# Expert stage of a hybrid decoder layer: the down products of a tile are placed between the two halves of the next tile's gate and up products

## What is computed

```python
g_sel = argmax(h @ w_group + b)            # one of 4 groups per token
top_v, top_i = top_k(e_in, 2)              # two of the 4 experts of that group
hg = einsum('td,edf->tef', t, w_gate)      # 1024 -> 256 per expert
hu = einsum('td,edf->tef', t, w_up)        # 1024 -> 256 per expert
act = silu(hg) * hu * comb
out = einsum('tef,efd->td', act, w_down)   # 256 -> 1024 per expert
return h + out
```

## Time and profile before

| what | value |
|---|---|
| median of 3 runs | 1578.01 us (1574.78 to 1580.17) |
| profiled execution, its own time | 1579.26 us |
| span of that execution in the trace | 1577.2 us |
| PE busy over the span | 1460.0 us, 93% |
| DVE busy | 1093.0 us, 69% |
| ACT busy | 770.2 us, 49% |
| first transposes of an activation (tile 0), start | 1245.40 us |
| transposes of the activation of tile 29, start | 1547.69 us |
| last product of the kernel, start | 1561.24 us |

### The profile page before, as it was taken

The page is one execution under the profiler, slowest core; times in us unless marked ns, Lnnn a source line. Parts: engine busy times, 40 slices in busy tenths (PEclk is TensorE's granted clock), DMA queues, the critical chain, the costliest instruction groups (busy, mean ns, idle before and its releaser), DMA issues.

```text
span 1577.2 us, 19883 instructions
## 1 busy us (share of the span) xinstructions
PE 1460.0 (93%) x7190; PEld 1208.0 (77%) x7190; DVE 1093.0 (69%) x1527; ACT 770.2 (49%) x1271; POOL 499.2 (32%) x365
## 2 busy tenths in 40 slices
PE   5999999999999888999999999999995789989894
PEld 5987888987889676677678888888874677878773
DVE  4328999999999957765569833347335788878873
ACT  5248223426332626766343442233244577867773
POOL 2310222374214143000335533322340334534421
PEclk9998999999999997999999999999997799999998
DMA  5200121113211022210355343443435788797775
GB/s 191 64 27 1 42 49 38 34 49 106 82 39 48 28 92 68 61 34 27 89 183 164 94 147 140 147 152 106 173 131 206 271 279 266 187 332 243 226 205 129
DMA packets 87216, 195.19 MB, mean 124 GB/s; under 512 B 11088, under 2 KB 32848, under 8 KB 84816
## 3 DMA queue, kind: packets, MB, share of 16 engines
q1 hardware_dynamic: 74448, 153.56, 29.1%
q0 software_dynamic: 8928, 32.51, 8.6%
q10 hardware_dynamic: 3744, 7.87, 1.3%
HBM read 200.71 MB, written 37.22 MB: 151 GB/s over the span
## 4 chain that ended last, share of the span: by engine, by line
PE 74%; DVE 9%; DMA 8%; ACT 4%; issue 3%; SPq 1%; POOL 1%; ACTq 0%; DVEq 0%; POOLq 0%
PE ps L721 21%; PE ps L722 20%; PE ps L723 20%; PE ps L947 4%; DMA e_raw<-in_w_up 3%; DMA out<-e_y,dest 2%; PE ps L937 2%; DVE e_lo L1983 2%; PE ps L1056 1%; DMA w_raw<-in_w_in 1%; DVE dist L1605 1%; PE ps L877 1%; DMA xin<-in_x 1%; DVE f_sum L1716 1%; PE ps L890 1%
## 5 line engine op out<-in xcount | busy, mean ns | idle before, releaser
L2040 POOL TENSOR_TENSOR w_lo<-w_raw,w_hi 128x512 fp32r<-128x512 f32 (+1 forms) x184 | 258.2, 1408 | 611.9 <-ACT w_hi L1124 611.2
L1124 ACT CAST w_hi<-w_raw 128x512 fp32r<-128x512 f32 (+1 forms) x184 | 112.2, 615 | 409.1 <-PE ps L723 356.4
L721 PE MATMUL ps<-w_hi,n_hi 128*128 128x512 f32 (+2 forms) x704 | 244.4, 347 | 1.9 <-ACT ro L1285 1.6
L723 PE MATMUL ps<-w_hi,n_lo 128*128 128x512 f32 (+2 forms) x704 | 242.1, 344 | 0.0
L722 PE MATMUL ps<-w_lo,n_hi 128*128 128x512 f32 (+2 forms) x704 | 241.9, 344 | 0.0
L1983 DVE TENSOR_TENSOR e_lo<-e_raw,e_hi 128x2048 fp32r<-128x2048 f32 x93 | 210.1, 2286 | 30.9 <-ACT e_hi L1495 30.6
L1495 ACT CAST e_hi<-e_raw 128x2048 fp32r<-128x2048 f32 x93 | 176.2, 1915 | 69.3 <-DMA e_raw<-in_w_up 69.3
L1642 DVE MAX8 small<-dist 128x8 f32<-128x384 f32 (+5 forms) x192 | 171.8, 895 | 6.6
L1643 DVE MATCH_REPLACE8 dist<-small,dist 128x384 f32<-128x384 f32 (+5 forms) x192 | 168.1, 876 | 0.0
L721 PE MATMUL ps<-n_hi,w_hi 128*128 128x512 f32 x416 | 164.1, 394 | 2.7 <-POOL w_lo L2040 2.6
L722 PE MATMUL ps<-n_lo,w_hi 128*128 128x512 f32 x416 | 162.3, 390 | 0.0
(11 more groups left out here) (272 smaller groups left out, 2875.4 us busy)
## 6 DMA issues: line engine op xcount, KB each, us to landing
e_raw<-in_w_gate SPq DMA_DIRECT2D x62, 512.0 KB
e_raw<-in_w_up SPq DMA_DIRECT2D x62, 512.0 KB
e_raw<-in_w_down SPq DMA_DIRECT2D x31, 1024.0 KB
w_raw<-in_w_in SPq DMA_DIRECT2D x120, 256.0 KB, 2.7
a_raw<-att_dram SPq DMA_DIRECT2D x16, 512.0 KB, 3.4
a_raw<-ret_dram SPq DMA_DIRECT2D x16, 512.0 KB, 3.4
w_raw<-in_w_out SPq DMA_DIRECT2D x24, 256.0 KB, 3.4
w_raw<-in_w_in SPq DMA_DIRECT2D x40, 128.0 KB, 2.3
```

The source lines that it names most:

```text
L721: mm(out, a[0], b[0], start=first, stop=False, skip_group_check=skip)
L723: return mm(out, a[1], b[0], start=False, stop=last, skip_group_check=skip)
L1124: nc.scalar.copy(w_hi[c % NH][:, :width], split_from(c)[:, :width]).then_inc(hi_ready, 1)
L2040: G.tensor_tensor(w_lo[c % NH][:, :width], split_from(c)[:, :width], w_hi[c % NH][:, :width].bitcast(F32), ALU.subtract).then_inc(lo_ready, 1)
```

## The change

PE's `gate_up(i)` is cut in two: `gate_up(i, 0)` does k = 0..3 and `gate_up(i, 1)` k = 4..7, and `down(i-1)` stands between the two. On ACT and DVE the split of part 2 of tile i moves ahead of the activation of tile i, and the split of part 1 of tile i+1 moves behind it on ACT (on DVE it stood there already). No instruction is added or removed, SP's and POOL's code is unchanged.

```diff
-            def gate_up(i):
+            def gate_up(i, half):
                 b = i.parity
-                pe.wait_ge(exT_lo, i.n + 1)
-                if i.reached(1):
-                    pe.wait_ge(gu_read, i.n)
-                for k in range(KT):
+                if half == 0:
+                    pe.wait_ge(exT_lo, i.n + 1)
+                    if i.reached(1):
+                        pe.wait_ge(gu_read, i.n)
+                for k in range(4 * half, 4 * half + 4):
...
-                last.then_inc(gu_full, 1)
+                if half:
+                    last.then_inc(gu_full, 1)
...
                 if not i.reached(NTILE):
-                    gate_up(i)
+                    gate_up(i, 0)
                 if i.reached(1):
                     down(i - 1)
+                if not i.reached(NTILE):
+                    gate_up(i, 1)
             each_step(work, NTILE)
...
                     x_part(i + 1)
+                w_part(i, 2)
+                if not (i + 1).reached(NTILE):
                     w_part(i + 1, 0)
-                    w_part(i + 1, 1)
                 act.wait_ge(gu_full, i.n + 1)
                 if i.reached(1):
                     act.wait_ge(gu_read, i.n)
                 A(gated[:], ps[:, B_GU:B_GU + FF], ACT.Silu).then_inc(gu_silu, 1)
-                w_part(i, 2)
+                if not (i + 1).reached(NTILE):
+                    w_part(i + 1, 1)
...
                     x_part(i + 1)
+                w_part(i, 2)
+                if not (i + 1).reached(NTILE):
                     w_part(i + 1, 0)
                 dve.wait_ge(gu_silu, i.n + 1)
...
                 V.tensor_tensor(arow[:], gated[:], ps[:, B_GU + FF:B_GU + 2 * FF], ALU.mult).then_inc(gu_read, 1)
                 if not (i + 1).reached(NTILE):
                     w_part(i + 1, 1)
-                w_part(i, 2)
```

## The result

| | before | changed |
|---|---|---|
| median, us | 1577.29 (6 runs, 1574.78 to 1580.17) | 1586.2 (6 runs, 1584.18 to 1586.95) |
| profiled execution, us | 1579.26 | 1585.08 |
| its span, us | 1577.2 | 1583.1 |

The ratio of the changed kernel to the kernel before is 1.0054, with a 95% interval of 1.0040 to 1.0068: slower by 8.9 us between the medians (6.3 to 10.7 by the interval), 6.1 were forecast. (The six runs of before contain the three that the prediction had.)

What follows compares the result with a forecast made beforehand. PE was taken as the bound, waiting for `arow` behind late transfers. 29 steps of 10.60 us gave +5.1, start +0.5, end +0.5: in all +6.1, a median of 1584 us, range 1579 to 1595.

Steps and rivals of the forecast that it cites:

- What bounds the kernel, and what the change takes away: Expert stage: PE sets the end; late weight transfers delay `arow`; nearly all of 31.4 us excess should go.
- under 25: ACT's waits for weight transfers were to fall from 69 us to under 25, 15 of the 69 ahead of the stage.
- What it adds: PE before the activation transposes: nothing hides the way over Silu and `arow`; 1.32 us where 0.23 would do, every tile.
- some 29: PE's waits at the transposes of nearly all 31 activations, about 1 us each, some 29 us in total.
- The step, 10.60: PE's step per tile in the expert stage: 10.55 us, or 10.65 if PE stops before the down products; 10.60 taken.
- The start, +0.5: DVE has one more weight part, 2.20 us, ahead of tile 0's `arow`, where it idled 1.73 us: +0.5 us.
- The end, +0.5: After tile 29's transposes: `e_y` stands behind Silu 30 on ACT, so the last add starts at 18.1, not 17.5: +0.5 us.
- Rival 1: `at_lo` comes in time, PE never stops ahead of the down products: step 10.55, +4.2 us, 1582 us; chance 0.22.
- Rival 2: Row transposes pass the waiting activation transposes on PE, so DVE sets the step: -6.9 us, 1571 us; chance 0.07.
- the DVE floor: DVE in the expert stage: `arow` could follow in a step of 10.15 us at the least, 0.4 us to spare.
- Rival 3: Weight transfers stay late, 12.9 us of transfers in a 10.6 us step: +16 us, 1600, or half, 1592; chance 0.15.
- rival 4: PE's clock swings between its levels from brief idling, a drop in every second step: +25 us, 1609 us; chance 0.06.

Runs made afterwards that it cites:

- before without loads: The kernel before with the expert weight loads of tiles 2 to 30 left out, output not that of the reference: 1546.02 us, one run.
- PE's order alone: Kernel before with only PE's change, down products between the two gate halves, ACT and DVE as before: 1612.25 us, ratio 1.0231.
- late down products: Changed kernel with the down products placed behind six of the eight gate k instead of four: 1581.61 us, ratio 1.0024.
- the kernel without loads: Changed kernel with the expert weight loads of tiles 2 to 30 left out, output not that of the reference: 1585.97 us, one run.
- part order alone: Kernel before with only the new order of weight parts on ACT and DVE, PE's gate products whole: 1555.77 us, ratio 0.9875.
- the kernel with `at_hi` and `at_lo` first: Changed kernel with `at_hi` on ACT and `at_lo` on DVE moved ahead of the split of part 1: 1607.95 us, ratio 1.0187.

## Why the prediction was right, and where it was off

- **What bounds the kernel, and what the change takes away: right.** The 31.4 us were late transfers (before without loads: 270.88 us), and the changed kernel loses at most 0.6 us to them. ACT's transfer waits fell to 14.8 us, all ahead of the stage, against "under 25"; the steps are alike but for the first.
- **What it adds: right.** The transposes come 0.90 us after the Silu's start, forecast 0.89, the first gate product at 2.06 (2.05), `at_lo` ends at 4.84 (4.82). The waits sum to 29.8 us at 31 tiles, "some 29" had been said. Its whole price, measured without loads, is 37.7 us; the prediction's terms give 36.5. (The prediction's last sentence calls gain and loss "both near 31 us", which its own sum does not bear out for the loss; that PE's order alone costs 28.8 us is no support for it either, see above.)
- **The step, 10.60: mis-sized by 0.07.** I had 10.55 for a PE that runs through and 10.65 for one that stops, and took the middle. It stops in every step but the first, since the two arrivals (4.84 plus the signal, against 4.90) are the same each time; the stop costs 0.13, not 0.10 (late down products: 10.53 without it). Over the stage that is 28 steps 0.067 too long and one 0.07 too short, 1.8 us, which is what it is longer than the forecast's 307.4. Which side of 0.02 us PE would fall on, the rows of before could not tell; the middle was a choice and no reading.
- **The start, +0.5: right, +0.39.** The table has +0.96 for it, but its stretch begins at the last gate product of tile 0, and that one came earlier in the changed kernel's execution for a reason of its own. The granted clock was still 0.50 for the first five of the 24 gate products of tile 0 before, and for the first two now. The first gate product before, then the first and the last of them and `arow` in the changed kernel:

```profile
1237.61 0.77 PE L721 MATMUL ps<-e_hi,x_hi 128*128 128x512 f32 x1
```

```profile
1235.46 0.77 PE L721 MATMUL ps<-e_hi,x_hi 128*128 128x512 f32 x1
...
1241.36 0.39 PE L723 MATMUL ps<-e_hi,x_lo 128*128 128x512 f32 x1
...
1243.17 0.41 DVE L2019 TENSOR_TENSOR arow<-gated,ps 128x256 f32<-128x256 f32 x1
```

From the first gate product to the transposes it is 1245.40 - 1237.61 = 7.79 us before and 1243.64 - 1235.46 = 8.18 now. In seven kernels of the study with the new part order this stretch is 8.17 or 8.18 us, whether the gate products of tile 0 took 5.74 or 6.17 (with 6.97, in the late down products, it is 8.29): DVE sets it, with the part that stands ahead of `arow`. The prediction's 2.20 - 1.73 = 0.47 was that.
- **The end, +0.5: +0.75.** The last add started 18.2 us after tile 29's transposes (1571.02 - 1552.84), forecast 18.1; before 17.5. The last 0.1 lies behind the add.

```profile
1564.27 1.55 POOL L2179 DMA_INDIRECT out<-e_y,dest  x1 [6.25 <-ACT e_y L1511]
...
1571.02 1.55 POOL L2179 DMA_INDIRECT out<-e_y,dest  x1 [5.20 <-DMA out<-e_y,dest]
```

- **Rival 1** (halves in time, 1582) fell, but narrowly: the late down products are that rival made true, and they gave 1581.61 with steps of 10.53, for which it had 10.55. **Rival 2** rested on the DVE floor, which was wrong; and when the row transposes really did pass the wait, the step stayed 10.67, so its condition (0.4 us of the wait hidden) did not decide either, because `at_lo` was as late. **Rival 3** fell with the kernel without loads, **rival 4** with the clock of 1.00 over all 29 steps.
- The forecast of the sign held because gain and loss were each known to within 2 us (31.4 and 31.4; 36.5 and 309.20 - 270.88 = 38.3). That the part order alone is worth 21 us stood in the prediction's numbers only half: the false floor hid from me that the gain could be had without the loss, at steps of 9.34 us.

## What to carry to other kernels

When a change moves two orders at once, price each engine's order by itself: here the order in which buffers come free (the same as that in which one queue refills them) was worth 25.7 us and the split of the products cost 32.6, and only the first was wanted. Before work is moved away from between a producer's last product and the step that needs its result over two other engines, look for what else fills that gap; if nothing does, the bare way is paid every time. An idle time in a schedule drawn up by hand is no floor until one has let the operation ahead of it slide.

## What the runs showed of the hardware

- Regular waits of PE of 0.93 us, one in every step of 10.67 (29 in the stage), left the granted clock at 1.00 over 309.20 us. So did longer ones: about 1.75 us in nearly every step of 11.36 of the kernel with `at_hi` and `at_lo` first.
- The length of one wait does not tell whether the clock falls. In the kernel before it fell to 0.50 after a wait of 2.26 us, which followed waits of 0.86 and 2.00 us in the two steps ahead of it, and after the longest; it stayed at 1.00 after others of 2.27, 2.28 and 3.06 us, and in the part order alone after one of 3.00 us.
- A weight load that waits 0.25 us costs the step 0.13 us: the first product after such a stop takes 0.49 to 0.50 us where others take 0.39, and the next one starts 0.33 us after it in place of 0.23.
- At the end of the kernels, where no loads run, adds to `out` that wait for each other come every 6.6 to 7.0 us; beside loads they wait up to 9.7 us each in the part order alone, and up to 11.1 in the changed kernel.
